# Hybrid two-layer backbone on one core: the second expert's weights loaded from the projection on, routing scratch in two chunks, token lists as four partial sums, padding rows left out of gathers

## The reference: what is computed

```python
glog = (xt @ w_group + b_group).astype(jnp.float32)
_, g_sel = lax.top_k(glog, 1)
elog_g = jnp.take_along_axis(elog, g_sel[:, :, None], axis=1)[:, 0]
e_val, e_idx = lax.top_k(elog_g, TOP_K)                 # TOP_K = 2
weights = g_w * jax.nn.softmax(e_val, axis=-1)
...
hdn = jax.nn.silu(xb @ w1[e]) * (xb @ w3[e])            # per expert: D 1024 -> FF 512
return hdn @ w2[e]                                      # 512 -> 1024
...
y = ys[dest] * flat_w[order][:, None]
return jax.ops.segment_sum(y, tok, num_segments=N)
```

## Time and profile before

| | |
|---|---|
| median of 3 runs | 2707.2 us (2703.96 to 2710.78) |
| profiled execution, its own time | 2706.1 us |
| its span, first to last instruction | 2704.3 us |
| TensorE busy | 2494.7 us, 92% of the span |
| VectorE busy | 1211.8 us, 45% |
| mean granted TensorE clock | 0.962 |
| moved by DMA | 640.07 MB, mean 237 GB/s |

### The profile page before, as it was taken

One profiled execution on the slowest core, in us unless ns is written; L12 is line 12 of the kernel. 1 busy time (PEld: TensorE's weight loads), 2 busy tenths in 40 slices (PEclk: granted clock), 3 DMA queues, 4 the chain that ended last, 5 costly groups with the idle time before them and its releaser, 6 DMA issues. The chain is left out here.

```text
span 2704.3 us, 64097 instructions
## 1 busy us (share of the span) xinstructions
PE 2494.7 (92%) x26358; PEld 1674.0 (62%) x26358; DVE 1211.8 (45%) x2786; ACT 689.7 (26%) x1427; POOL 449.5 (17%) x550
## 2 busy tenths in 40 slices
PE   7999999999989969999999489999999699999884
PEld 6888788788854546777765284555445476554542
DVE  3234333433455463222222256566575655554445
ACT  4222322322330002333323355335320000000002
POOL 0012111111122102222212220000011122221112
PEclk9999999999999969999999799999999799999997
DMA  6323223223164369999999851011044799999998
GB/s 270 117 92 118 100 85 118 99 78 123 48 244 156 125 255 407 414 415 414 414 415 414 322 200 44 16 47 31 22 183 156 306 413 414 414 415 415 415 415 318
DMA packets 126859, 640.07 MB, mean 237 GB/s; under 512 B 18272, under 2 KB 30976, under 8 KB 70736
## 3 DMA queue, kind: packets, MB, share of 16 engines
q1 hardware_dynamic: 94960, 539.66, 50.5%
q0 software_dynamic: 17024, 54.54, 5.4%
q10 hardware_dynamic: 14688, 43.08, 4.0%
HBM read 575.27 MB, written 61.95 MB: 236 GB/s over the span
## 5 line engine op out<-in xcount | busy, mean ns | idle before, releaser
L1759 PE MATMUL PS<-wt,xT 128*32 128x256 f32 x11648 | 677.5, 383 | 39.9 <-DMA wt<-in_w 34.0
L1759 PEld LDWEIGHTS PS<-wt,xT 128*32 128x32 f32 x11648 | 415.8, 111 | 267.0 <-DMA wt<-in_w 35.4
L1774 PE MATMUL PS<-wt,hidT 128*32 128x256 f32 x5824 | 356.7, 384 | 9.3 <-issue 7.3
L724 PE MATMUL PS<-hT,slab 128*128 128x256 f32 x1280 | 296.0, 385 | 6.3 <-DVE low L617 3.5
L1839 DVE STREAM_TRANSPOSE xT<-xg 128x256 f32<-128x256 f32 x186 | 82.9, 446 | 479.9 <-PE PS L1759 470.8
L1774 PEld LDWEIGHTS PS<-wt,hidT 128*32 128x32 f32 x5824 | 209.6, 111 | 121.4 <-issue 16.4
L724 PEld LDWEIGHTS PS<-hT,slab 128*128 128x128 f32 x1280 | 239.8, 192 | 42.9 <-issue 6.5
L437 POOL TENSOR_SCALAR prob<-prob,inv 128x640 f32<-128x640 f32 (+2 forms) x80 | 130.1, 1626 | 662.5 <-DVE inv L632 662.5
L1687 ACT ACTIVATE u<-PS 128x128 f32<-128x128 f32 x186 | 51.6, 277 | 709.7 <-PE PS L1759 687.6
L1646 POOL DMA_INDIRECT xg<-h_d,ib x192 | 188.3, 981 | 151.0 <-POOL ib L1643 147.9
L515 ACT ACTIVATE prob<-prob,low 128x640 f32<-128x640 f32 (+2 forms) x160 | 117.6, 735 | 300.3 <-DVE low L617 300.2
(11 more groups left out here) (300 smaller groups left out, 2787.4 us busy)
## 6 DMA issues: line engine op xcount, KB each, us to landing
wt<-in_w SPq DMA_DIRECT2D x256, 1024.0 KB
wt<-in_w2s SPq DMA_DIRECT2D x128, 1024.0 KB
aw<-in_ada_w SPq DMA_DIRECT2D x48, 1024.0 KB, 5.0
ys_d<-y ACTq DMA_DIRECT2D x184, 128.0 KB, 5.3
slab<-in_slabs SPq DMA_DIRECT2D x24, 512.0 KB, 3.3
tab<-in_tables SPq DMA_DIRECT2D x8, 1408.0 KB, 7.3
ys_d<-zero POOLq DMA_DIRECT2D x4, 2560.0 KB, 9.4
x_d<-x_p ACTq DMA_DIRECT2D x18, 512.0 KB, 5.1
```

The source lines that it names most:

```text
L724: mm = pe.matmul(W[HALF[n]], slab[m][:, k, :], hT[:, k, c * PW:(c + 1) * PW], start=(k == 0), stop=(k == KD - 1))
L1759: mm = t.matmul(PS[32 * g:32 * g + 32, UP, 0:QD], xT[:, k * 32:k * 32 + 32], wt[b][:, q, c * 1024 + g * QD:c * 1024 + g * QD + QD], start= ...
L1774: mm = t.matmul(PS[32 * g:32 * g + 32, DOWN, 0:QD], hT_[:, k * 32:k * 32 + 32], wt[b][:, q, c * 1024 + g * QD:c * 1024 + g * QD + QD], sta ...
```

## The change

Four edits, all around the start of the expert stage.

1. `Projection.stream` gets a helper `second(q)` for expert 1 into slot 1. Layer 0: chunks 0 and 1 once the x1 rows are stored, chunk 2 once the h rows are stored, chunks 3 and 4 once the last logits are there. Layer 1: chunks 4 and 5 as soon as the token tiles are requested, then 0, 1 and 2 in the same three steps. One chunk (5 in layer 0, 3 in layer 1) stays in the expert stage, now ahead of the merge's small loads.
2. The routing scratch that lives long is kept in two chunks of slot 3, with `OHi0` moved to the memory of `xg` 2, 3 and `y`. The expert of place 3 is then loaded in steps: chunks 4 and 5 after `tab_ok` as before, 2 and 3 after the first half of the masks, 0 after `idx_ok`, 1 after the chain's table.
3. Each tile's list product is made once, in column group n mod 4, so the four groups hold partial sums (40 and 32 matmuls instead of 160 and 128). VectorE copies them out (`listed`), and four more matmuls with `quarters` add them into every group. `idx` moves ahead of the chain's table in VectorE's stream.
4. Token numbers are kept minus 2048, so that a padding row gets an index beyond the tensor. The gather has a bounds check that leaves such rows out; `xg` 0 and 1 are cleared first.

The diff, cut to its core:

```diff
+NOWHERE = 2048
...
+            FREE, BY_ROWS, BY_STORES, BY_LOGITS, LEFT = ((), (4, 5)), ((0, 1), (0,)), ((2,), (1,)), ((3, 4), (2,)), ((5,), (3,))
...
+                def second(q):
+                    view = A["w13"][l, 1, q] if q < 4 else A["w2s"][l, 1, q - 4]
+                    sp.dma_start(wt[1][:, q, :], view).then_inc(self.w_in[1][q], 16)
+
+                for q in self.FREE[l]:
+                    second(q)
+
                 def third(q):
                     view = A["w13"][l, 2, q] if q < 4 else A["w2s"][l, 2, q - 4]
                     sp.dma_start(wt[2][:, q, :], view).then_inc(self.w_in[2][q], 16)
@@ -902,8 +911,19 @@
                 third(3)
                 sp.wait_ge(self.h_ok, self.nt)
                 third(5)
+                for j in range(2):
+                    sp.wait_ge(self.x_out[j], 8 * self.nt)
+                for q in self.BY_ROWS[l]:
+                    second(q)
+                for j in range(2):
+                    sp.wait_ge(self.h_out[j], 8 * self.nt)
+                sp.wait_ge(self.tr_ok, self.nt)
+                for q in self.BY_STORES[l]:
+                    second(q)
                 sp.wait_ge(self.rl_ok, self.nt)
                 third(4)
+                for q in self.BY_LOGITS[l]:
+                    second(q)
...
-                    a.dma_start(self.y[2 * KD * w:2 * KD * (w + 1), 0:P],
+                    a.dma_start(self.rows[2 * KD * w:2 * KD * (w + 1), :],
...
+            xT, u, hid, hT_ = (small(f"{x}_{l}", [P, w]) for x, w in (("xT", QD), ("u", P), ("hid", P), ("hidT", P)))
+            lent = small.at + 4 * 2 * QD
             xg = [small(f"xg_{l}{j}", [P, QD]) for j in range(DEEP)]
-            xT, u, hid, hT_ = (small(f"{x}_{l}", [P, w]) for x, w in (("xT", QD), ("u", P), ("hid", P), ("hidT", P)))
             y = small(f"y_{l}", [P, D])
+            assert lent + 4 * nt * ITEMS <= small.at
+            OHi0 = at(f"OHi0_{l}", lent, [P, nt, ITEMS])
...
-                assert RING_AT + 4 * carved[0] <= SCR_AT
+                assert carved[0] <= 2 * CHUNK
...
-            pos, rank = (T(1) for _ in range(2))
+            pos, rank, quarters, listed = T(1), T(1), T(STRIP), T(ITEMS)
             soon, in_second, in_block, token = T(nt, 2), T(nt), T(nt), T(nt)
+            tokm, qcolm = T(nt), T(1)
...
-            OHt, OHi, idf = T(NA, STRIP), T(NA, ITEMS), T(ITEMS)
+            OHt, OHi1, idf = T(NA, STRIP), T(nt, ITEMS), T(ITEMS)
+            OHi = OHi0, OHi1
+            late_at = RING_AT + 4 * carved[0]
+            bndf, past_places, hit, chainf, j32 = T(EXPERTS + 3), T(EXPERTS), T(EXPERTS), T(EXPERTS), T(EXPERTS)
+            is_last, kth, place_k = (T(1) for _ in range(3))
+            assert late_at >= RING_AT + 4 * CHUNK
...
+                    for q in Projection.LEFT[l]:
+                        chunk(1, 1, q)
                     merge.early_loads(sp)
-                    for q in range(NCH):
-                        chunk(1, 1, q)
                     sp.wait_ge(tab_ok, 2)
                     e = sp.value_load(ert[0:1, FIXED:FIXED + 1], min_val=0, max_val=EXPERTS - 1)
                     for q in range(4, NCH):
                         chunk_at(e, FIXED, q)
+                    sp.wait_ge(e_ok, 1)
+                    sp.wait_ge(masks, 4)
+                    for q in (2, 3):
+                        chunk_at(e, FIXED, q)
                     sp.wait_ge(idx_ok, 2)
-                    for q in range(4):
-                        chunk_at(e, FIXED, q)
+                    chunk_at(e, FIXED, 0)
+                    sp.wait_ge(masks, 7)
+                    chunk_at(e, FIXED, 1)
...
-                    sp.wait_ge(masks, 6)
...
-                    g.memset(idx[:, ITEMS:ITEMS + DEEP], 0).then_inc(pad_ok, 1)
+                    g.memset(idx[:, ITEMS:ITEMS + DEEP], 4 * NOWHERE).then_inc(pad_ok, 1)
+                    for j in range(2):
+                        g.memset(xg[j][:, :], 0.0).then_inc(pad_ok, 1)
+                    g.wait_ge(pad_ok, 3)
...
-                                             in_offset=bass.IndirectOffsetOnAxis(ap=ib[:, j:j + 1], axis=0)).then_inc(g_in[j], 16)
+                                             in_offset=bass.IndirectOffsetOnAxis(ap=ib[:, j:j + 1], axis=0),
+                                             bounds_check=4 * N - 1, oob_is_err=False).then_inc(g_in[j], 16)
...
-                    g.wait_ge(pad_ok, 1)
...
-                            for g in range(4):
-                                mm = t.matmul(PS[32 * g:32 * g + 32, 2, 0:ITEMS], OHt[:, n, :], OHi[:, n, :],
-                                              start=(n == 0), stop=(n == NA - 1))
+                            g = n % 4
+                            mm = t.matmul(PS[32 * g:32 * g + 32, 2, 0:ITEMS], OHt[:, n, :], OHi[k][:, n - k * nt, :],
+                                          start=(n < 4), stop=(n >= NA - 4))
+                    mm.then_inc(summed, 1)
+                    t.wait_ge(masks, 6)
+                    for g in range(4):
+                        mm = t.matmul(PS[32 * g:32 * g + 32, 2, 2 * ITEMS:3 * ITEMS], quarters, listed, start=True, stop=True)
                     mm.then_inc(summed, 1)
...
+                    link(v.tensor_scalar(tokm, tok, -float(NOWHERE), None, ALU.add))
+                    link(v.tensor_scalar(qcolm, qcol[:, :], 4.0 * NOWHERE, None, ALU.add))
+                    link(v.tensor_reduce(quarters, ident[:, :].rearrange("p (g c) -> p c g", c=STRIP), AX, ALU.add))
...
-                    link(v.tensor_tensor(token, tok, A2[:, 0:nt, 0], ALU.mult))
+                    link(v.tensor_tensor(token, tokm, A2[:, 0:nt, 0], ALU.mult))
...
-                                             expand(tok, (2, STRIP)), ALU.mult))
-                        v.tensor_tensor(OHi[:, k * nt:k * nt + nt, :], expand(itm[:, k, :], (2, ITEMS)),
+                                             expand(tokm, (2, STRIP)), ALU.mult))
+                        v.tensor_tensor(OHi[k][:, :, :], expand(itm[:, k, :], (2, ITEMS)),
                                         expand(iot, (1, nt)), ALU.is_equal).then_inc(masks, 1)
                     rows_T(0, 0, 0)
                     link(v.tensor_copy(dst[:, :, 0:nt], df))
+                    v.wait_ge(summed, 5)
+                    v.tensor_copy(listed, PS[:, 2, 0:ITEMS]).then_inc(masks, 1)
...
+                    v.wait_ge(summed, 6)
+                    link(v.tensor_scalar(idf[:, 2:ITEMS], PS[:, 2, 2 * ITEMS + 2:3 * ITEMS], 4.0, qcolm, ALU.mult, ALU.add))
+                    v.tensor_copy(idx[:, 2:ITEMS], idf[:, 2:ITEMS]).then_inc(idx_ok, 1)
...
-                    v.wait_ge(summed, 5)
-                    link(v.tensor_scalar(idf[:, 2:ITEMS], PS[:, 2, 2:ITEMS], 4.0, qcol[:, :], ALU.mult, ALU.add))
-                    v.tensor_copy(idx[:, 2:ITEMS], idf[:, 2:ITEMS]).then_inc(idx_ok, 1)
```

More of the change, by code:

```diff
@@ L1155, in __init__, with begin @@
                 self.gcol, self.scol, self.ncol = (mods("gcol0", [P, 2, KD]), mods("scol0", [P, 2, KD]), mods("ncol0", [P, KD]))
-            def begin(self, ys_ok, y):
-                self.ys_ok, self.y = ys_ok, y
+            def begin(self, ys_ok, rows):
+                self.ys_ok, self.rows = ys_ok, rows
                 nm = lambda x: sem(f"{x}_c0")
@@ L1217, in early_tensor @@
                 t.wait_ge(self.cols_in, 48)
-                t.matmul(PS[:, 5, 0:4 * KD], self.y[0:4 * KD, 0:P], ident[0:4 * KD, 0:4 * KD], start=True, stop=True
+                t.matmul(PS[:, 5, 0:4 * KD], self.rows[0:4 * KD, :], ident[0:4 * KD, 0:4 * KD], start=True, stop=True
                          ).then_inc(self.turned, 1)
@@ L1538, in T @@
                 carved[0] += n
-                assert RING_AT + 4 * carved[0] <= SCR_AT
+                assert carved[0] <= 2 * CHUNK
                 names = "abcd"[:len(shape)]
                 return ap.rearrange(f"p ({' '.join(names)}) -> p {' '.join(names)}", **dict(zip(names, shape)))
-            OH, A2, A2c, gl, m4, goh, _, _, oh0, oh1, (_, gsum, _, v0, v1) = scratch(nt)
+            OH, A2, A2c, gl, _, goh, _, _, oh0, oh1, (_, _, _, best0, best1) = scratch(nt)
+            m4, gsum, v0, v1 = T(nt, GROUPS), T(nt), T(nt), T(nt)
             prod, prb = T(2, nt, EXPERTS), T(nt, EXPERTS)
-            base, one32, j32 = (T(EXPERTS) for _ in range(3))
+            base, one32 = T(EXPERTS), T(EXPERTS)
             blk, key, k31d = (T(EXPERTS + 1) for _ in range(3))
-            pos, rank = (T(1) for _ in range(2))
+            pos, rank, quarters, listed = T(1), T(1), T(STRIP), T(ITEMS)
             soon, in_second, in_block, token = T(nt, 2), T(nt), T(nt), T(nt)
+            tokm, qcolm = T(nt), T(1)
             gt, Z, H = T(EXPERTS), T(EXPERTS), T(EXPERTS)
-            bndf, npf, past_places = T(EXPERTS + 3), T(1), T(EXPERTS)
-            is_last, single, least, over, itc, bm, kth, place_k = (T(1) for _ in range(8))
-            delta, hit, chainf, beyond = T(EXPERTS), T(EXPERTS), T(EXPERTS), prod[:, 0]
```

(9 more changed lines are left out.)

## The result

The changed kernel takes 2688.86 us in the median of 4 runs (2687.67 to 2690.05) against 2707.45 for the kernel before (2703.96 to 2710.78). The ratio is 0.9931 [0.992, 0.9943]: 18.6 us faster, where 17.5 were forecast.

A forecast was written before the change was run, and what follows sets the result against it. DMA bounds layer 1's experts, DMA and TensorE those of layer 0. Layer 0's 8.0 us (7.0 + 2.1 - 1.1) and layer 1's 9.5 (loads 6.5 + gathers 3.0) make 17.5: 2689.7 us from 2707.2, range 2683 to 2699.

The forecast's parts named there:

- The sum: Both layers: 8.0 us gained in layer 0 and 9.5 in layer 1, together 17.5, from 2707.2 to 2689.7 us.
- Gathers: Expert stages: padding rows left out partly relieve DMA, gaining 3.0 us in layer 1 and 1.5 in layer 0.
- the lower is 0: Expert stages: skipping padding rows may gain 0 us, as the slowest engine ends a load and padding fills high rows.
- Rival (a): Expert stages: no relief from left-out padding rows; layer 1 keeps 6.5 us, layer 0 8.0; -14.5, 2692.7 us; chance 0.31.
- rival (b): Expert stages: full relief from left-out padding rows, -23 us in all, 2684 us; chance 0.13.
- The bound: Expert stages: upper limit of gain if every engine lost its part, 7.6 us in layer 1, 3.1 in layer 0.
- Loads: Start of reloads: earlier expert chunks fill resting DMA, giving loads 6.5 us more lead in either layer (4.4 to 7.6).
- DMA should hardly rest before the reloads: Sign before the reloads: early loads fill DMA's resting time, about 4.4 + 2.6 us, and short rests earlier.
- Lists: Stage start, layer 0: first `up` at 1009.2, 2.5 us earlier; item 1 2.1 earlier, less 1.1 for the clock.
- Layer 0 as a gate: Layer 0 near 1108.91: waiting for a freed slot limits the reload's gain to 5.7 us; the stall needs 6.2 to vanish.
- Rival (c): Stage start: early loads eaten up by SP's waits or delayed gathers, low clock costs 3.6 us; about 6 left, 2701; chance 0.10.
- Rival (d): POOL: gathers with bounds check much slower, deciding from 4.2 us each; at 5 us, 76 us in layer 0; chance 0.08.

The follow-up runs named there:

- spread and reversed padding: Changed kernel with each item's padding dealt evenly over its strip of 32 places, or put on the first places: 2685.79 and 2689.91 us.
- Loads alone: Changed kernel with lists made four times, padding rows read and no bounds check: 2703.82 us, 4.0 faster than the kernel before.
- gathers alone: Kernel before with only the gathers' edit (padding rows point outside, bounds check): 2696.02 us, 11.2 faster than the kernel before.
- the added ones: Changed kernel with 120 unread TensorE products before the first mask, meant to keep the clock up: 2720.26 us.

## Why the prediction was right, step by step

**The sum was right by errors that cancel.** Forecast were 8.0 in layer 0 and 9.5 in layer 1; the stages gave 7.0 and 12.7, and 1.3 were lost again behind the second one. That last stretch is 47.1 to 48.6 us long in all the profiles here, whatever the kernel, so part of this 1.3 is scatter. In layer 0 the 8.0 was reached, 8.1 at the `up` of 1411.77 (0.3 of it from ahead of the stage), but a new stall at 1471.86 and the last items gave 0.8 back, which the sum had at nothing. That the total came within 1.1 us is luck in part: layer 1 gained 3.2 more than forecast.

**Gathers, 3.0 and 1.5: too small by half.** Undoing them costs 6.1 and 2.9, adding them alone gives 7.7 and 4.9. The step that failed is "the lower is 0, as the end of a load is the end of its slowest engine, and padding always fills the high rows of a strip of 32": I took a middle between it and the average. The runs with spread and reversed padding show that the place of padding in the strip decides nothing, so the average was the right price. By the Trainium skill, "DMA: Bandwidth & Descriptors", "The descriptor swizzle", which states the mapping for a 1 MiB transfer to 128 partitions, the engines of the first rows would have got little relief; this case's runs don't agree with that reading for these gathers of 128 KB (layer 1's stage: 519.6 us with padding first, 519.6 spread, 519.3 last). Whether their rows are not tied to engines by place, or the weights don't wait for the slowest engine, no run here separates. Rival (a) is refuted and rival (b) was right about its mechanism. The bound itself was read a little high: by the last stall the gathers' megabytes had fallen by 19% (10.10 to 8.15), not by the 26.4% of all items; 0.19 x 0.063 x 457 is 5.5 us, and the two runs measured 6.1 and 7.7. That the second equals the bound of 7.6 is chance in part.

**Loads, 6.5 in either layer: alone 5.1 in layer 1, in layer 0 less.** What I didn't separate are its halves. Expert 1's earlier chunks, taken away alone, cost nothing in the median (3 us in the one layer 1 stage profiled); place 3's, put back behind the lists, cost 10.7. The sentence "DMA should hardly rest before the reloads" was wrong in layer 1: 3.1 us at 2134 to 2138, more than the 2.6 that it was to fill. I had counted the resting time before and what fills it, and not what would be in the queue while SP waits for the masks. At the start of the reloads one chunk is left to issue as I said, and the term's size fits what was measured: 5.1 alone and 2.3 of the lists (below) are 7.4 where 6.5 was forecast with `idx` 2.1 earlier.

**Lists.** First `up` 2.6 us earlier, 2.5 forecast; in layer 1 at 22.78 instead of 25.20 after the stage's start, 2.4. The 20 records behind the second mask took 1.65 us, 83 ns each, where 54 ns and 1.1 us were forecast; the mask itself came some 0.3 earlier. Item 1 came 1.1 earlier (1.0 forecast, 2.1 less 1.1), and the low clock took 1.4. The sum had no term of its own for the lists in layer 1, only the earlier `idx` within the loads; the run without the short lists shows what that is worth there, 2.3 us. The order of `idx` and table, which I had priced as a delay of one chunk alone, costs 2.3 us at item 1 when the lists are long (7.6 us from item 0 to item 1 instead of 5.3).

**Layer 0 as a gate.** The rest of DMA at 1106 came as worked out, and SP issued at 1107.94, 1.0 earlier, as TensorE frees the slot. The prediction had 2.1 there: it left its own 1.1 for the clock out of the lead (5.7) and of the lead needed (6.2) alike, so that their comparison stood. The stall's 7.0 us can be won once. Loads alone remove it, gathers alone win 6.0 of its 7.0 (0.84 us of waiting stay), so terms that each removed it must not be added; the prediction didn't add them there. The gathers' 2.9 us in the changed kernel's layer 0 lie mostly at another place, the last items, where waits for weights appear when rows are read.

**Rival (c)** had the right suspicion about one half of the loads and lost by the lists and gathers. **Rival (d)**: 1038 ns instead of 978, far from 4.2 us. The q0 row fell by 11.5%, outside the 15 to 25% given: it holds more than these gathers.

## What to carry to other kernels

An early load is worth the time in which DMA would rest, and only if the queue still has work when the next gate (a mask, a list, a freed slot) holds it back: follow the queue to that gate before pricing the load. Where a stage runs at the pace of DMA, bytes left out anywhere count at the average of the engines until a run shows otherwise, and stage lengths show microseconds that the medians of whole runs blur. When a list gets shorter, look at what the engine that waited for it did meanwhile, and size extra work by a row of the same operands, counted in calls of the program and not in records of the profile.

## What the runs showed of the hardware

A gathered row left out by the bounds check is not a packet left out: q0 has 17024 packets before and after, and only the megabytes fall. The check costs 55 ns of POOL's time for each gather of 128 rows (1036 against 981 ns), whether or not rows are left out. The float32 products counted here (lists, `up`, the added ones) stood as two records each. An added product of 128 moving columns and 32 stationary ones took about 236 ns (2 x 118), even with the clock granted at 1.00 for most of it; a list product of 144 moving columns took 166 ns (2 x 83) on the half clock, and 108 (2 x 54) in the kernel before. Two differences are in view and neither was tested: the added products all write to one group of 32 columns, where successive list products go to different ones, and their weight loads (PEld) fill 5.00 of the 5.00 us of the window above, against 2.45 of 3.00 in the earlier trace rows. Why they differ stays open.
